# Token-major weight chunks computed in pairs, with 256 weight columns per product, in a transformer kernel on one core

## What is computed

```
q, k, v, g, z = jnp.split(xn @ w_in, GLA_SPLITS, axis=-1)          # gated linear attention: v is 1024 wide
k, v = jnp.split(rms_norm(h, kv_norm) @ w_kv, [1024], axis=-1)     # differential attention: v is 1024 wide
q = rms_norm((xn @ w_q).reshape(B, S, DIFF_HEADS, 2, DIFF_DH), q_gain) * (DIFF_DH ** -0.5)
v = proj[..., OFF_V:OFF_GATE]                                      # window attention: v is 256 wide
kv = mem_h @ w_kv                                                  # memory: k and v, 1024 wide each
```

## Time and profile before

| | before |
|---|---|
| median of 3 runs | 1771.71 us (1768.76 to 1771.73) |
| span of the profiled execution, first to last instruction | 1765.0 us |
| the profiled execution's own time | not listed apart; the three runs are 3.8 to 6.7 us above the span |
| mean granted clock of PE | 0.935 |
| PE busy | 1591.4 us, 90% |
| DVE busy | 1138.0 us, 64% |
| ACT busy | 891.7 us, 51% |
| POOL busy | 290.2 us, 16% |
| moved by DMA | 233.69 MB, mean 132 GB/s |

### The profile page before, as it was taken

How to read it: one execution, slowest core, us unless ns; L and a number is a source line. 1 busy time by engine, 2 the same in 40 slices (tenths; PEclk the granted TensorE clock), 3 DMA queues, 4 the chain that set the end, 5 groups by cost and what they waited for, 6 DMA issues and landing times. The chain is left out here.

```text
span 1765.0 us, 32384 instructions
## 1 busy us (share of the span) xinstructions
PE 1591.4 (90%) x12184; PEld 1374.6 (78%) x12184; DVE 1138.0 (64%) x1769; ACT 891.7 (51%) x1699; POOL 290.2 (16%) x333
## 2 busy tenths in 40 slices
PE   6996999988998999989877769898989989789999
PEld 4885888877885888879766657787867877678888
DVE  4585666674454666764999965656667556457665
ACT  4333544455345544445766665454455355354443
POOL 3000301030000311122755500001200003021111
PEclk9998999998796999988988989999989989899999
DMA  6220455544621455543333332223524324235552
GB/s 271 96 96 24 148 187 191 182 151 111 152 73 46 147 190 190 176 151 116 131 107 108 119 108 84 98 94 120 176 93 160 122 96 145 71 122 190 190 175 88
DMA packets 35313, 233.69 MB, mean 132 GB/s; under 512 B 3840, under 2 KB 6912, under 8 KB 7936
## 3 DMA queue, kind: packets, MB, share of 16 engines
q1 hardware_dynamic: 30816, 223.75, 35.9%
q10 hardware_dynamic: 3216, 4.19, 1.5%
q0 software_dynamic: 1168, 4.20, 0.8%
HBM read 227.93 MB, written 4.19 MB: 132 GB/s over the span
## 5 line engine op out<-in xcount | busy, mean ns | idle before, releaser
L362 PE MATMUL ps<-xa_hi,w_hi 128*128 128x256 f32 x1680 | 626.6, 378 | 85.0 <-DVE w_lo L1387 27.3
L1387 DVE TENSOR_TENSOR w_lo<-raw,w_hi 128x1024 bf16<-128x1024 f32 x420 | 538.6, 1282 | 192.1 <-ACT w_hi L864 189.8
L864 ACT CAST w_hi<-raw 128x1024 fp32r<-128x1024 f32 x420 | 437.8, 1044 | 355.8 <-PE ps L364 174.6
L364 PE MATMUL ps<-xa_bf,w_lo 128*128 128x256 bf16 x1680 | 492.2, 293 | 0.0
L363 PE MATMUL ps<-xa_lo,w_hi 128*128 128x256 f32 x1680 | 478.6, 285 | 0.0
L362 PEld LDWEIGHTS ps<-xa_hi,w_hi 128*128 128x128 f32 x1680 | 352.0, 209 | 96.3 <-issue 80.4
L363 PEld LDWEIGHTS ps<-xa_lo,w_hi 128*128 128x128 f32 x1680 | 339.5, 202 | 0.5
L362 PE MATMUL ps<-xb_hi,w_hi 128*128 128x256 f32 x704 | 261.1, 376 | 17.6 <-DVE xb_lo L1400 6.7
L390 PE MATMUL ps<-xb_hi,w_hi 128*128 128x256 f32 x768 | 274.0, 363 | 0.0
L364 PEld LDWEIGHTS ps<-xa_bf,w_lo 128*128 128x128 bf16 x1680 | 165.4, 98 | 72.1
L392 PE MATMUL ps<-xb_bf,w_lo 128*128 128x256 bf16 x768 | 217.0, 283 | 0.0
(11 more groups left out here) (270 smaller groups left out, 2384.9 us busy)
## 6 DMA issues: line engine op xcount, KB each, us to landing
raw<-weights SPq DMA_DIRECT2D x210, 1024.0 KB, 4.8
band<-arena ACTq DMA_DIRECT2D x1, 3072.0 KB, 34.7
arena<-band POOLq DMA_DIRECT2D x8, 256.0 KB, 3.2
arena<-gla_masks SPq DMA_DIRECT2D x1, 1088.0 KB, 15.0
H<-x_t SPq DMA_DIRECT2D x1, 1024.0 KB, 4.8
arena<-mem_t POOLq DMA_DIRECT2D x1, 1024.0 KB, 5.2
arena<-band POOLq DMA_DIRECT2D x8, 128.0 KB, 2.7
out_t<-H ACTq DMA_DIRECT2D x8, 128.0 KB, 2.0
```

The source lines that it names most:

```text
L362: mm(ps[:, bank, 0:T], w_hi[:, s, k], X.hi[:, k], start=k == 0, stop=False)
L364: last = mm(ps[:, bank, 0:T], w_lo[:, s, k], X.bf[:, k], start=False, stop=k == KC - 1)
L864: nc.scalar.copy(w_hi[:, j % HI_SLOTS].rearrange("p k n -> p (k n)"), raw[:, j // 2 % RING, j % 2]).then_inc(hi_done, 1)
L1387: TT(w_lo[:, j % HI_SLOTS].rearrange("p k n -> p (k n)"), raw[:, j // 2 % RING, j % 2], w_hi[:, j % HI_SLOTS].rearrange("p k n -> p (k n)" ...
```

## The change

The 26 chunks are taken as 13 pairs. `token_half(c)` computes one token tile of both chunks of a pair at once: the X block of that tile is stationary, and 2 x 128 weight columns, 128 of either chunk, stream past it. The even half (t = 0) does tile 0, the odd one tile 1. A half has 24 products, 16 of fp32r and then the 8 of bf16, and fills one bank with 256 columns. Both halves wait until both chunks are cut, and `gemm_done` is raised by 2 behind the second; a new count, `token_done`, tells DVE of the first. `tokens` empties a half with one instruction of 256 columns. In differential attention the order becomes two Q, two V, two Q, ... (`Q_AT` = 0, 1, 4, 5, 8, 9, 12, 13; `two_turns` orders the weights to match), so head sums, squares and norms move with Q. `diff_rstd` gets a buffer of its own, `d_ln`, in place of `lnt`. The calls for the window attention's and the memory's V are changed in the same way.

```diff
--- before.py
+++ after.py
@@ -73,6 +73,7 @@
+Q_AT = [i for i in range(2 * DIFF_HEADS) if i % 4 < 2]
...
@@ -270,7 +272,7 @@
-        gemm_done = sem("gemm_done")
+        gemm_done, token_done = sem("gemm_done"), sem("token_done")
...
@@ -347,32 +349,44 @@
         def _(pe):
             mm = nc.tensor.matmul
 
-            def chunk(c, j, X, build, token_major=False, banks=BANKS):
+            def chunk(c, j, X, build, banks=BANKS):
 
                 s, bank = j % HI_SLOTS, j % banks
                 pe.wait_ge(hi_done, c + 1)
                 pe.wait_ge(lo_done, c + 1)
                 if not isinstance(c, int) or c >= banks:
                     pe.wait_ge(bank_free, c - banks + 1)
-                if not token_major:
-                    for k in range(KC):
-                        if build is not None:
-                            pe.wait_ge(X.bf_done, KC * build + k + 1)
-                            pe.wait_ge(X.lo_done, KC * build + k + 1)
-                        mm(ps[:, bank, 0:T], w_hi[:, s, k], X.hi[:, k], start=k == 0, stop=False)
-                        mm(ps[:, bank, 0:T], w_hi[:, s, k], X.lo[:, k], start=False, stop=False)
-                        last = mm(ps[:, bank, 0:T], w_lo[:, s, k], X.bf[:, k], start=False, stop=k == KC - 1)
+                for k in range(KC):
+                    if build is not None:
+                        pe.wait_ge(X.bf_done, KC * build + k + 1)
+                        pe.wait_ge(X.lo_done, KC * build + k + 1)
+                    mm(ps[:, bank, 0:T], w_hi[:, s, k], X.hi[:, k], start=k == 0, stop=False)
+                    mm(ps[:, bank, 0:T], w_hi[:, s, k], X.lo[:, k], start=False, stop=False)
+                    last = mm(ps[:, bank, 0:T], w_lo[:, s, k], X.bf[:, k], start=False, stop=k == KC - 1)
+                last.then_inc(gemm_done, 1)
+
+            def token_half(c, X, build, banks=BANKS):
+
+                t = c % 2
+                first, bank = c - t, c % banks
+                s = slice(first % HI_SLOTS, first % HI_SLOTS + 2)
+                at = slice(t * P, (t + 1) * P)
+                pe.wait_ge(hi_done, first + 2)
+                pe.wait_ge(lo_done, first + 2)
+                pe.wait_ge(bank_free, c - banks + 1)
+                if build is not None:
+                    pe.wait_ge(X.bf_done, KC * build + KC)
+                    pe.wait_ge(X.lo_done, KC * build + KC)
+                to = ps[:, bank, 0:T].rearrange("p (s n) -> p s n", s=2)
+                for k in range(KC):
+                    mm(to, X.hi[:, k, at], w_hi[:, s, k], start=k == 0, stop=False)
+                    mm(to, X.lo[:, k, at], w_hi[:, s, k], start=False, stop=False)
+                for k in range(KC):
+                    last = mm(to, X.bf[:, k, at], w_lo[:, s, k], start=False, stop=k == KC - 1)
+                if t == 0:
+                    last.then_inc(token_done, 1)
                 else:
-                    if build is not None:
-                        pe.wait_ge(X.bf_done, KC * build + KC)
-                        pe.wait_ge(X.lo_done, KC * build + KC)
-                    for t in range(NT):
-                        at = slice(t * P, (t + 1) * P)
-                        for k in range(KC):
-                            mm(ps[:, bank, at], X.hi[:, k, at], w_hi[:, s, k], start=k == 0, stop=False)
-                            mm(ps[:, bank, at], X.lo[:, k, at], w_hi[:, s, k], start=False, stop=False)
-                            last = mm(ps[:, bank, at], X.bf[:, k, at], w_lo[:, s, k], start=False, stop=k == KC - 1)
-                last.then_inc(gemm_done, 1)
+                    last.then_inc(gemm_done, 2)
 
             def half_chunk(c, j, half, build):
 
@@ -479,7 +493,10 @@
                     for c in (8 + 2 * u, 9 + 2 * u):
-                        chunk(c, c, XA, None, token_major=c < C_GG)
+                        if c < C_GG:
+                            token_half(c, XA, None)
+                        else:
+                            chunk(c, c, XA, None)
                     decays(u)
                 if u:
                     scores(u - 1)
@@ -529,12 +546,12 @@
 
                 if i < 2 * DIFF_HEADS:
                     c = C_DVQ + i
-                    if i % 2 == 0:
-                        chunk(c, c, XA, None, token_major=True, banks=2)
+                    if i in Q_AT:
+                        chunk(c, c, XB, XB_DQ if i == 0 else None, banks=2)
                     else:
-                        chunk(c, c, XB, XB_DQ if i == 1 else None, banks=2)
-                if i % 2 == 0 and 2 <= i <= 2 * DIFF_HEADS:
-                    head_sums(DIFF_HEADS + i // 2 - 1)
+                        token_half(c, XA, None, banks=2)
+                if i - 1 in Q_AT:
+                    head_sums(DIFF_HEADS + Q_AT.index(i - 1))
 
             def diff_scores(u):
                 h, t = u // 2, u % 2
@@ -731,7 +748,10 @@
-                    chunk(c, c, X, build, token_major=S_V <= m < S_Q or m >= S_XV, banks=2)
+                    if S_V <= m < S_Q or m >= S_XV:
+                        token_half(c, X, build, banks=2)
+                    else:
+                        chunk(c, c, X, build, banks=2)
                 if m - 1 in S_NORMED:
                     head_sums(HN_K + S_NORMED.index(m - 1))
                 if S_XK < m <= S_XV and (m - S_XK) % 2 == 0:
@@ -1011,12 +1031,11 @@
             def v_or_q(i):
                 if i < 2 * DIFF_HEADS:
                     cut_hi(C_DVQ + i + AHEAD, C_DVQ + i + AHEAD)
-                h = i // 2 - 1
-                if 0 <= h < DIFF_HEADS:
-                    if i % 2 == 0:
-                        head_sq(DIFF_HEADS + h, C_DVQ + 2 * h + 1, d_q[:, h])
-                    else:
-                        head_rstd(DIFF_HEADS + h)
+                if i - 1 in Q_AT:
+                    h = Q_AT.index(i - 1)
+                    head_sq(DIFF_HEADS + h, C_DVQ + i - 1, d_q[:, h])
+                if i - 2 in Q_AT:
+                    head_rstd(DIFF_HEADS + Q_AT.index(i - 2))
 
             def diff_sq(i):
                 act.wait_ge(da["o"], 2 * i + 2)
@@ -1405,12 +1424,17 @@
 
                 TT(to, got(c, j, banks), rstd[:], ALU.mult).then_inc(bank_free, 1)
 
-            def tokens(c, j, to, r, banks=BANKS):
-
-                dve.wait_ge(gemm_done, c + 1)
-                for t in range(NT):
-                    ins = TS(to[:, t], ps[:, j % banks, t * P:(t + 1) * P], r[:, t:t + 1], None, ALU.mult)
-                ins.then_inc(bank_free, 1)
+            pairs = [0]
+
+            def tokens(c, to, r, banks=BANKS):
+
+                t = c % 2
+                if t == 0:
+                    pairs[0] += 1
+                    dve.wait_ge(token_done, pairs[0])
+                else:
+                    dve.wait_ge(gemm_done, c + 1)
+                TS(to[:, t], ps[:, c % banks, 0:T], r[:, t:t + 1], None, ALU.mult).then_inc(bank_free, 1)
 
             def residual(c0, X, build, gain):
                 for n in range(8):
@@ -1524,7 +1548,8 @@
                         if c < C_GG:
-                            tokens(c, c, g_v[:, :, (c - C_GV) * P:(c - C_GV + 1) * P], rtok)
+                            at = (c - C_GV) // 2 * T
+                            tokens(c, g_v[:, :, at:at + T], rtok)
                         else:
                             scaled(c, c, g_gate[:, c - C_GG])
             dve.wait_ge(ga["s"], 2 * GLA_HEADS + 1)
@@ -1571,14 +1596,14 @@
             def v_or_q(i):
                 if i < 2 * DIFF_HEADS:
                     c = C_DVQ + i
-                    h = i // 2
                     cut_lo(c + AHEAD, c + AHEAD)
-                    if i % 2 == 0:
-                        tokens(c, c, d_v[:, :, h * P:(h + 1) * P], rtok, banks=2)
+                    if i in Q_AT:
+                        scaled(c, c, d_q[:, Q_AT.index(i)], banks=2)
                     else:
-                        scaled(c, c, d_q[:, h], banks=2)
-                h = i // 2 - 2
-                if i % 2 == 0 and 0 <= h < DIFF_HEADS:
+                        h = i // 4 * 2
+                        tokens(c, d_v[:, :, h * P:(h + 2) * P], rtok, banks=2)
+                if i - 3 in Q_AT:
+                    h = Q_AT.index(i - 3)
                     head_out(DIFF_HEADS + h, d_q[:, h], gains[:, 2:3])
 
             for i in range(DVQ_AHEAD):
@@ -2098,13 +2124,16 @@
     def turns(a, b):
 
+    def two_turns(a, b):
+        return [c for n in range(0, len(a), 2) for c in a[n:n + 2] + b[n:n + 2]]
+
     a, b = x["a_w_in"][0], x["w_in_2"][0]
...
-    out += kv[0:8] + turns(kv[8:16], cut(x["b_w_q"][0])) + cut(x["b_w_out"][0]) + mlp(x["mlp_w1"][1], x["mlp_w2"][1])
+    out += kv[0:8] + two_turns(cut(x["b_w_q"][0]), kv[8:16]) + cut(x["b_w_out"][0]) + mlp(x["mlp_w1"][1], x["mlp_w2"][1])
```

More of the change, by code:

```diff
@@ L216, in program @@
         d_lp = cut(2, DIFF_DH)
+        d_ln = cut(2, T)
         w_row = cut(BAND, rows=SWA_HEADS)
@@ L393, in half_chunk, with chunks @@
                 last.then_inc(gemm_done, 1)
```

(11 more changed lines are left out.)

2 lines of the change are left out of this document (1 added, 1 removed).

## The result

| | before | changed |
|---|---|---|
| median beside each other | 1770.24 us (4 runs, 1767.61 to 1771.73) | 1713.05 us (4 runs, 1707.88 to 1714.86) |
| ratio | | 0.9679, 95% interval 0.9661 to 0.9698 |
| profiled execution: time | not listed apart | 1713.74 us |
| profiled execution: span | 1765.0 us | 1711.8 us |
| mean granted clock | 0.935 | 0.943 |

The change is faster by 3.2%; the forecast was 1716 (1706 to 1735). Between the two profiled spans lie 53.2 us, between the medians 57.2. Twice more, on other occasions, the same pair gave 1767.64 to 1714.65 (0.9692, 0.9645 to 0.9739) and 1767.36 to 1715.04 (0.9701, 0.9676 to 0.9726): 53 and 52 us.

A forecast was written before the change was run, and what follows sets the result against it. PE (TensorE), busy 90% of the span, was taken as the bound. Gains of 15.4 (GLA), 25.4 (differential attention), 3.8 (V pair) and 11.2 (memory) sum to 55.8 us; 1771.7 less that gives 1716 us, range 1706 to 1735.

The forecast's parts named there:

- Product cost: All 26 chunks: a half takes 2.85 us like an ordinary chunk, instead of 4.78, a plain gain of 50 us.
- GLA: Gated linear attention, 4 steps: each falls from 13.06 to 9.21 us with no new waits, gaining 15.4 us.
- Differential attention: Its 8 V chunks: prologue 9.7, steps 0 and 1 6.9, four later chunks 7.4, tail 1.4; gain 25.4 us.
- The clock part: Differential attention: clock back near the first Q chunk's end; prologue 30.2 to 20.5 us, steps 0 and 1 17.1 to 10.2.
- four later V chunks at full clock: 4 x 1.86: Differential attention after steps 0 and 1: each of four V chunks gains 1.86 us, together 7.4 us.
- The line on the tail: End of differential attention: head 7's sums come before the tail, less 0.6 us for step 9's later half; gain 1.4 us.
- The slabs: Weight queue in differential attention: faster chunks ask sooner, but the slab is needed seven chunks on; cost nothing.
- V pair: Window attention's V pair: PE busy throughout, gain about 2 x 1.9 = 3.8 us.
- Memory: Memory's 8 V fillers in window attention: gross 15.2 us, less 1.1 pair sums, 0.8 pace, 2.1 last cut; gain 11.2.
- the clock comes back no sooner: Differential attention's two clock falls last as long as before; some 8 us less gain, 1724 us, chance 0.17.
- late release makes DVE the bound: Seven pairs inside the attention loops: 2.7 us of cut and evacuation each on the path; 19 us lost, 1735, chance 0.11.
- The other two: Pairs wait for their own cuts, 1776 us, chance 0.04; weights moving in two pieces take twice as long, about 1771, 0.03.

The follow-up runs named there:

- the run with 128 columns: The changed kernel with each half computed as two groups of 24 products of 128 columns; 1765.07 us, 0.9983 of the kernel before.
- the run with the order alone: The changed kernel with the old 48-product form in all 26 chunks, leaving only Q, Q, V, V and `d_ln`; 1767.05 us, 1.0004 of the kernel before.
- the run with the head norm moved: The changed kernel with `diff_rstd` and `diff_head` ahead of the filler's cut and the last memory cut behind step 15's maximum; 1712.82 us, 0.9680 of the kernel before.

## Why the prediction was right, and where it was wrong

- **Product cost: right.** 2.84 us a half against 2.85. But two terms behind it cancel, neither of them in the sum. With alternating types a half takes 2.95, so the half as such is 0.1 us dearer than the ordinary chunk, and the bf16 products at the end give it back. The lower bound had priced the order at 10 ns a product; it gives about half of that. The estimate of 2.6 us a half, from the Trainium skill's figure for a product alone (page "TensorE: Matmul & The Clock Gate", section "Back-to-back issue gap"), isn't reached in the changed kernel; GLA's shortest half takes 2.79.
- **GLA: right.** 15.8 against 15.4, in every run with this pair. No wait, as forecast; DVE carries steps of 9.1 to 9.4 us (7.3 for the first, where it took 11.3 before).
- **Differential attention: one step wrong, 25.4 against 18 to 20.4.** The clock part held: the prologue took 21.3 us (422.14 to 443.40) against 20.5, steps 0 and 1 took 9.2 against 10.2. The step that failed is "four later V chunks at full clock: 4 x 1.86", which had no wait in it: the products gain those 7.4 us, and 5.5 of waits and 0.5 of smaller delays stand against them. The line on the tail had the delay of u = 9's second half as 0.6 at the maximum of u = 11; it showed as one of the waits of 1.70, ahead of the transposes of u = 10. The late release was priced as a rival "for the buffers of the weights", and argued away because PE has two fillers before it needs them. PE never waited for a weight. It waited for ACT's and DVE's other work, which stands in program order behind the cut that waits for the pair's end: 5.5 us in all. Moving that work ahead of the cut shows it (the waits go from where they stood, 4.0 us up to the transposes of u = 10), and so do the run with 128 columns, which has pairs and such waits, and the run with the order alone, which has neither. Over the whole stretch only 1 to 1.6 us come back, since the next link is late then.
- **The slabs: right.** No wait for a weight's arrival in this stretch.
- **V pair: right**, 3.9 against 3.8. The 2.5 us behind it were not foreseen; they make up for a third to a half of what differential attention lacks.
- **Memory: right**, 10.9 against 11.2, in its terms too. The pair-sum wait, taken at 1.1, stood at 1.63 at L743. The uncovered last cut, taken at 2.1, is 2.8 - 0.75 = 2.0 in the rows above; moving it away gave 2.5. The pace term, taken at 0.8, showed as one wait of 0.51 for a bank.
- **Rival "the clock comes back no sooner": refuted**, by the windows above: some 5 us instead of 13. What brings it back is open: with the order alone it stays down through two full chunks of 128-column products, but in the run with 128 columns it rose between two halves. Its price was rounded up too: two places of two and a half chunks at 2.1 us are 10.5, of which the sum had charged 3.7 already, so 6.8 instead of "some 8".
- **Rival "late release makes DVE the bound", 19 us: wrong in size.** It has three places of 1.7 to 2.5 us (two in differential attention, one at the end of the window loop) and three waits of 0.6 to 0.9, and none in GLA. DVE is the bound nowhere: it waits for ACT's rounding, and ACT for the pair.
- **The other two** (the pair waits for its own cuts; two pieces are no faster): no trace has a wait of over 0.53 us ahead of a half, and a half takes 2.84 us.
- **The sum** was 55.8 and the spans lie 53.2 apart: 5.0 us missing in differential attention against 2.6 behind the V pair that nobody had foreseen. The median came out at 1713.05, 3 below the forecast, because the base was too high as well. The first trace of the kernel before was a quick execution, of nearly 1767 us (span 1765.0 and the 1.9 us by which the changed kernel's time exceeds its span), 4.8 below the 1771.7 to which the sum was applied; the kernel's medians on the later occasions are 1766.83, 1767.64 and 1767.36. That the medians of the result lie 57.2 apart, where 53 and 52 came later, and that the time came out so near to the forecast, is in part luck.

## What to carry to other kernels

When the same arithmetic can be had with fewer, wider products, don't price a product by its columns alone: half the products at twice the columns took 59% of the time here (2.84 of 4.78 us). That the rest of a product's time is its weight load was argued from the rows and not tested by itself. When a change makes a resource come free later and in larger lumps, the user of the resource may be well served and the loss stand elsewhere: list what the engine that waits for it has queued behind that wait, and put what doesn't need the resource ahead. To price such a step, compare places in the traces by the starts of a group that both kernels have, since whole times here differ by over 10 us between executions of one kernel.

## What the runs showed of the hardware

**The same program has a different clock from one execution to the next.** Outside the changed places the gain jumps between fixed values. Between cuts 335 and 351, in the memory attention, seven executions are within 0.4 us of the first one and six are 4.2 to 4.3 us faster, on the same instructions. The windows of that place in the changed kernel and in the run with the head norm moved:

```profile
1465.00:1469.00 4.00, 2.78 (x7) 2.24 (x8) 0.88 (x2) 0.25 (x1) 0.00 (x0) 0.50 0.02 4
```

```profile
1467.00:1471.00 4.00, 2.20 (x10) 1.97 (x11) 1.05 (x3) 0.80 (x2) 0.00 (x0) 1.00 0.01 4
```

The kernel before varies in the same way, from 1761.4 to 1771.8 us over the runs here, and the changed kernel from 1707.9 to 1720.6. What decides it isn't shown.

**A busy PE can lose its clock.** Behind the convolution's first chunk and its sums PE works on 32 products of 32 columns in plain float32 (L613, L614). In the changed kernel the clock is up when they begin and falls near 761.7 while PE has no idle time; it rises within the ordinary chunk behind them. PE's last long idle time, 3.62 us, had ended at 754.0, and that it has no part in the fall isn't shown. Windows:

```profile
758.00:762.00 4.00, 4.00 (x35) 3.96 (x34) 0.79 (x2) 1.14 (x4) 0.00 (x0) 0.93 0.55 205
764.00:768.00 4.00, 4.00 (x20) 4.00 (x21) 0.00 (x0) 0.00 (x0) 0.00 (x0) 0.50 0.00 0
```

In the kernel before it was down from the start of that stretch: from the first of these products (L596, L597) to the chunk behind them it took 13.7 us (791.06 to 804.72), here 10.7 (758.59 to 769.30). This is 3 of the 3.5 us by which the changed kernel gains between the cuts 188 and 200, in two executions of three, at a place that it doesn't touch.
